# Expert weight loads in runs of 8 KB per partition instead of two runs of 4 KB

## What is computed

```python
def expert_block(args):
    xb, e = args                                    # up to 128 tokens of one expert, width 1024
    hb = jax.nn.silu(xb @ w_gate[e]) * (xb @ w_up[e])
    return hb @ w_down[e]
```

## Time and profile before

| | |
|---|---|
| median of three executions | 1955.79 us (1955.04 to 1960.65) |
| the profiled execution, its own time | 1958.94 us |
| its span, first to last instruction | 1957.3 us |
| mean granted TensorE clock | 0.979 of full speed |
| PE busy | 1833.4 us (94%) |
| DVE busy | 1338.2 us (68%) |
| ACT busy | 847.4 us (43%) |
| DMA moved in all | 610.26 MB, mean 312 GB/s |

### The profile page before, as it was taken

How to read it: one execution, slowest core, us unless ns; L and a number is a source line. 1 busy time by engine, 2 the same in 40 slices (tenths; PEclk the granted TensorE clock), 3 DMA queues, 4 the chain that set the end, 5 groups by cost and what they waited for, 6 DMA issues and landing times.

```text
span 1957.3 us, 22496 instructions
## 1 busy us (share of the span) xinstructions
PE 1833.4 (94%) x8664; PEld 1306.3 (67%) x8664; DVE 1338.2 (68%) x1527; ACT 847.4 (43%) x939; POOL 222.8 (11%) x260
## 2 busy tenths in 40 slices
PE   7999999999999998889889998999999898889896
PEld 3788657778888656545657677578776566556654
DVE  4776679998789646534657888777696456445656
ACT  2324623223357535433546454444465345434553
POOL 3000110102032010001010200100020110011001
PEclk9999999999999999999999999999999999999998
DMA  9776426667399999999999777186699999999995
GB/s 351 271 238 242 136 74 197 241 218 278 112 345 363 410 409 407 402 406 403 398 402 361 282 260 270 41 290 248 224 376 388 409 409 408 407 402 399 400 389 208
DMA packets 179902, 610.26 MB, mean 312 GB/s; under 512 B 17001, under 2 KB 19253, under 8 KB 172753
## 3 DMA queue, kind: packets, MB, share of 16 engines
q1 hardware_dynamic: 150648, 503.62, 67.3%
q0 software_dynamic: 26192, 100.40, 14.6%
q10 hardware_dynamic: 2952, 4.77, 0.7%
HBM read 593.78 MB, written 27.33 MB: 317 GB/s over the span
## 4 chain that ended last, share of the span: by engine, by line
PE 72%; DMA 13%; DVE 10%; ACT 3%; issue 1%; SPq 1%; POOL 0%; ACTq 0%; DVEq 0%; POOLq 0%
PE bank L2641 62%; DMA ring<-in_w_exp_down_dram 9%; PE bank L3124 5%; PE bank L2651 3%; DVE work L1773 3%; DVE w_lo L1773 2%; ACT w_hi L1628 1%; DMA ring<-in_w_mod_dram 1%; DMA work<-hp_dram 1%; DVE m_lo L1773 1%; PE bank L2914 1%; DVE ring L1773 1%; DMA work<-in_w_mod_dram 1%; DMA x<-in_ctx_dram 1%; DMA ring<-in_w_out_dram 1%
## 5 line engine op out<-in xcount | busy, mean ns | idle before, releaser
L1773 DVE TENSOR_TENSOR w_lo<-ring,w_hi 128x2048 fp32r<-128x2048 f32 x228 | 519.4, 2290 | 273.4 <-ACT w_hi L1628 272.8
L1628 ACT ACTIVATE w_hi<-ring 128x2048 fp32r<-128x2048 f32 x228 | 436.9, 1919 | 238.0 <-PE bank L2641 131.1
L1352 ACT ACTIVATE m_hi<-ring 128x1024 fp32r<-128x1024 f32 (+1 forms) x128 | 130.0, 1031 | 265.2 <-PE bank L2641 223.1
L2641 PE MATMUL bank<-w_hi,xsT_hi 128*128 128x512 f32 x608 | 238.0, 391 | 3.5 <-DVE w_lo L1773 1.7
L2641 PE MATMUL bank<-w_lo,xsT_hi 128*128 128x512 f32 x608 | 236.8, 389 | 0.0
L3124 PE MATMUL bank<-ring,mixed 128*64 128x512 f32 x832 | 185.4, 598 | 7.8 <-DMA ring<-in_w_exp_up_dram 7.8
L1773 DVE TENSOR_TENSOR m_lo<-ring,m_hi 128x1024 fp32r<-128x1024 f32 (+1 forms) x128 | 148.8, 1188 | 57.3 <-ACT m_hi L1352 55.7
L2641 PE MATMUL bank<-w_hi,xsT_lo 128*128 128x512 f32 x608 | 187.3, 389 | 0.0
L2641 PE MATMUL bank<-m_lo,hT_hi 128*128 128x512 f32 (+1 forms) x496 | 186.3, 376 | 0.0
L2641 PE MATMUL bank<-w_hi,hexpT_hi 128*128 128x512 f32 x304 | 131.4, 432 | 56.0 <-DVE w_lo L1773 56.0
L2641 PE MATMUL bank<-m_hi,hT_hi 128*128 128x512 f32 (+1 forms) x448 | 170.5, 380 | 6.3 <-DVE m_lo L1773 4.4
(11 more groups left out here) (322 smaller groups left out, 2810.1 us busy)
## 6 DMA issues: line engine op xcount, KB each, us to landing
ring<-in_w_exp_gate_dram SPq DMA_DIRECT2D x128, 1024.0 KB, 12.9
ring<-in_w_exp_up_dram SPq DMA_DIRECT2D x128, 1024.0 KB, 13.3
ring<-in_w_exp_down_dram SPq DMA_DIRECT2D x128, 1024.0 KB, 12.6
ring<-in_w_in_dram SPq DMA_DIRECT2D x44, 1024.0 KB, 6.8
work<-in_w_mod_dram POOLq DMA_DIRECT2D x40, 1024.0 KB, 5.5
work<-hp_dram SPq DMA_DIRECT2D x54, 256.0 KB, 4.5
work<-mod_dram POOLq DMA_DIRECT2D x8, 1024.0 KB, 9.8
ring<-in_w_out_dram SPq DMA_DIRECT2D x8, 1024.0 KB, 5.3
```

The lines of the kernel that those rows point to most:

```text
L1352: nc.scalar.activation(high_of(key, q)[:, 0:n], ring[:, cols], ACT.Copy).then_inc(split_hi, 1)
L1628: nc.scalar.activation(w_hi[:, n % N_HIGH, :], raw(slot_of(n)), ACT.Copy).then_inc(hi_done, 1)
L1773: return nc.vector.tensor_tensor(o, a, b, op)
L2641: return nc.tensor.matmul(o, a, b, start=first, stop=last)
```

## The change

The source of a quarter is read as 256 rows in neighbouring pairs: rows 2p and 2p + 1 go to partition p, as one run of 8 KB that is contiguous in HBM and in SBUF. A quarter is then contiguous over all partitions. The weight block k of a quarter in the slot now has the rows of parity k. The transposed tokens and hidden rows have to match this, so the transposes of `xs` and `hexp`, and the matmuls of `place_first`, take every second column of a stretch of 256 (`paired`). The number and order of instructions on every engine stay as they are: PE, ACT, DVE, POOL and SP run the same lists.

```diff
@@ quarter_w
             rows = slice(2 * P * q, 2 * P * (q + 1))
             if isinstance(e, int):
-                return A[name][l, e, rows, :].rearrange("(k p) n -> p k n", k=2)
-            return A[name][l, bass.ds(e, 1), rows, :].rearrange("o (k p) n -> p (o k) n", k=2)
+                return A[name][l, e, rows, :].rearrange("(p k) n -> p (k n)", k=2)
+            return A[name][l, bass.ds(e, 1), rows, :].rearrange("o (p k) n -> p (o k n)", k=2)
@@ load, on SP
-                    sp.dma_start(raw(i).rearrange("p (k n) -> p k n", k=2),
+                    sp.dma_start(raw(i),
                                  quarter_w(l, EXPERT_W[p // 4], expert_in(e if p < 8 else e - 1), p % 4))\
                         .then_inc(slot_loaded[i], 16)
@@ on PE
+            def paired(row, j):
+
+                return row[:, 2 * P * (j // 2) + j % 2:2 * P * (j // 2 + 1):2]
+
+            def turn_paired(dst, src):
+
+                for j in range(4):
+                    ins = nc.tensor.transpose(dst[:, j * P:(j + 1) * P], paired(src, j), ident)
+                return ins
@@ turn_xs
-                        turn(bank[at + half], xs[:, par, half * 512:(half + 1) * 512], 4).then_inc(xt_mm, 1)
+                        turn_paired(bank[at + half], xs[:, par, half * 512:(half + 1) * 512]).then_inc(xt_mm, 1)
@@ place_first
-                                ins = mm(bank[2 + half][:, j * P:(j + 1) * P], h2row[k][:, kk * P:(kk + 1) * P],
+                                ins = mm(bank[2 + half][:, j * P:(j + 1) * P], paired(h2row[k], kk),
                                          place[0][:, k, :], k == 0, k == nt - 1)
@@ turn_h
-                        turn(bank[6 + half], hexp[:, half, :], 4).then_inc(ht_mm, 1)
+                        turn_paired(bank[6 + half], hexp[:, half, :]).then_inc(ht_mm, 1)
```

## The result

The changed kernel takes 1938.08 us in the median of four runs (1934.74 to 1941.83), against 1955.49 us (1955.04 to 1960.65) for the kernel before on the same chip. The figures in brackets are the lowest and the highest run. The medians differ by 17.4 us. The ratio, which goes by all runs, is 0.9906 with a 95% interval of 0.988 to 0.9931, that is 18.4 us less (13.5 to 23.5): under 1%, but clear of the noise. The forecast was 1931 us, 24.7 us less.

A forecast was written before the change was run, and what follows sets the result against it. The prediction took the DMA rate in the two expert stages as the bound. Saving 24.7 us on loads, with transposes and gather at nothing, gave 1934.2 us from the profiled 1958.9, or 1931 us against the median; range 1923 to 1940.

The forecast's parts named there:

- The bound: Expert stages, 605 to 996 and 1485 to 1877 us: DMA rate sets the pace, PE waits 15 us per pair.
- The mechanism: Weight loads in the expert stretches: each packet saved by 8 KB runs takes off 10.6 ns, raising 409 GB/s to 423.
- Rival A: Expert-stage loads: rate hardly rises, 423 GB/s belonging to the kernel's start; gain 0 to 8 us, 1948 to 1956; chance 0.12.
- The size of that term: Loads in both expert stretches: 0.085 us less per quarter over 290.4 quarters, 24.7 us less.
- The dips stay: Expert stretches: short rate dips come with gathers, scatters and other traffic and remain, so 24.7 us is taken, not 37.
- rival C: Expert stretches: dips shrink too, with fewer packets in play; 37 us less, 1918 us; chance 0.06.
- The transposes at nothing: Transposes' weight loads reading every second float: priced at nothing; upper end 140 ns more each, 30 us in all.
- the prediction's own sign: Weight load of `bank<-const,mixed`: stays at 140 ns; at 200 or more rival B holds and stretches outside the stage lengthen.
- rival B: 212 exposed loads outside the stretches: strided loads eat the gain; at 0.14 us each 1961 us, half slower 1946; chance 0.08.
- The gather: POOL's token gathers beside longer packets: up to 1.2 us more on 7.6 us, 20 us free, priced at nothing.
- 3 cycles per packet: Skill page's fixed packet cost on the DMA engine's bus: 3.5 ns per packet, 8 us in all; forecast used measured rates.
- The sum: Whole kernel: 1958.9 less 24.7 is 1934.2 us; against the median of three, 1931 us.

The follow-up runs named there:

- e1: Changed kernel with the two rows of each pair swapped in the slot, so packets are 4 KB again, strided transposes kept; 1958.57 us, ratio 1.0012 to the kernel before.
- m1: Separate kernel without the computation, streaming weights on SP's queue with various run lengths and depths; 387, 410, 422, 429 GB/s for 2, 4, 8, 16 KB.
- a0: The changed kernel run once more, no edit; 1940.17 us against 1956.85 for the kernel before, ratio 0.991.
- e5: Changed kernel with eight raw slots for quarters instead of nine; 1948.24 us, ratio 0.9958 to the kernel before.
- m2: Separate kernel without the computation, making 64 transposes or plain float32 matmuls per column step; transposes 7.0 us at step 1, 7.8 at step 2.
- e7: Changed kernel with runs of 16 KB, 2 MB per transfer into two neighbouring slots, eight slots in four pairs; 2055.09 us, ratio 1.0512 to the kernel before.

## Why the prediction was right, point by point, and where its size was off

- **The bound.** Right. The chain still goes through a down quarter in every pair, PE still waits there, and e1 shows that time follows the rate of the loads. But the reading that PE "has some 50 us of its own work in a pair and waits 15" is wrong: it took the DMA piece of the chain, which starts with the issue, for PE's wait. PE is busy for 59.6 us of a pair and idle for 6.0. The forecast held all the same, since the 2.0 us to be saved in a pair are less than 6.0 too; after the change 4.6 are left.
- **The mechanism, a fixed cost for each packet.** Right: e1 takes back the length of the run alone and the gain is gone; m1 gives one rate for each length, wherever the rows lie. Rival A, that 423 GB/s belongs to the start of the kernel, fell with the 420 GB/s of the stage.
- **The size of that term**, 0.085 us for a quarter and 24.7 us in all, was too large; this is the main slip. The step "423 GB/s against 409" took its upper figure from 9 us. Over long windows the loads alone give 422 against 410, 0.073 us and 21.1 us in all; in the stretches themselves the pair of profiles gave 10.7 + 10.1 = 20.8 us, and a0's 19.3. So 4 to 5 of the 6 to 8 us by which the forecast was off are here. The windows were to show 421 to 424 GB/s and show 420. That pairs take just the forecast 63.5 us is partly luck: 24 quarters at 0.073 us are 1.8 us, and 2.1 were saved; in a0's profile a pair takes 63.8.
- **The dips stay** (rival C had them shrink). Right: the wide phases are 2.4% under the full rate of 410 before, and 2.2% under 422 after. e5 shows that part of them is a short queue, since with eight slots the wide phases are at 407 instead of 413. How much comes from single slow packets was not separated.
- **The transposes at nothing** was wrong, though small: the price is 2.3 us (0.6 to 4.1) by e1. By the prediction's own sign ("if it reads 200 or more, B holds") rival B would have won, as the load reads 209 ns; yet the kernel is faster, and the piece behind 996 us, which was to become longer, is 1.9 us shorter. The sign was badly chosen: the length of a load is not its price. Rival B's upper end, 140 ns for each exposed load, was far off, as loads overlap. It also counted two kinds of load as one: of the 212, 116 are transposes, at 12 ns each by m2, and 96 are plain loads of `place_first`, at (15.2 - 14.4) / 128 = 6 ns each. That is 1.4 + 0.6 = 2.0 us, in line with e1. The Trainium skill, page "SBUF — State Buffer", note on SBUF cachelines, says that two hits in a line of 16 bytes are enough for full speed. For the plain load m2 agrees, with 196 ns at step 2 against 192. For the load of a transpose it takes 209 ns instead of 140, so there the measurement decides against it.
- **The gather.** Right, in its mechanism too. It was to land 1.2 us later and stay covered; it lands 9.2 us after its issue instead of 7.6, 1.6 later, and no gather is on the chain of the stage before or after. The cover is not endless: with runs of 16 KB (e7) the median for wide experts is 13.1 us, and one gather is on the chain, with 15.66 us.
- **The Trainium skill's 3 cycles per packet**, page "DMA: Bandwidth & Descriptors", section "Why small descriptors are slow (HBM only)", are an estimate of 3.5 ns at the 850 MHz of that page's section "Where 436 GB/s comes from". The first section names a second fixed cost, 32 bytes of descriptor metadata for each operation, which the estimate leaves out; at the 423 / 16 = 26 GB/s of one engine that is an estimate of 1.2 ns more. m1 shows 9 to 10 ns for each packet; the trace does not agree with the page, and the gain of 8 us that follows from the 3 cycles alone fell.
- **The sum.** Not closed to the microsecond. The stretches gave 20.8 us in one pair of profiles and 19.3 in the other, and what of the stride's price lies inside them is already in that. Taking off all of e1's 2.3 us leaves 17 to 18.5 us, against 17.6 and 18.4 by the two ratios; the agreement is closer than the intervals (13.5 to 23.5 in the first) can support, and single profiles vary by some 5 us in the mixer of layer 0.

## What to carry to other kernels

Where a row of the profile shows DMA engines busy all the time and PE waiting for loads, the length of the contiguous run per partition is worth measuring: price it with long windows of a transfer of that length, if the kernel has one somewhere, as this one had in its `w_mod` loads. Lay the data out so that the other side pays in work that is hidden; here strided transposes cost 2 us and the runs gave 20. Don't buy longer runs with coarser or fewer slots: one slot less cost 9 to 13 us, half or more of what doubling the run gave, and 16 KB runs in four large slots made the kernel 5% slower. And don't read a DMA piece of the chain as the time for which PE waits: here it was 15 us, and the wait 6.

## What the runs showed of the hardware

- Rate of loads from HBM on one queue, with nothing else running on the core: 387, 410, 422 and 429 GB/s for runs of 2, 4, 8 and 16 KB, with no difference between one contiguous piece and rows that lie apart (halves 512 KB apart at 4 KB, pieces 192 KB apart at 8 KB).
- Three 1 MB transfers in flight hold the full rate when nothing else runs, two don't (387 GB/s with 4 KB, 369 with 8 KB); in the kernel, with some four queued, the rate is still 2% short during the wide phases.
- An indirect gather beside such loads takes longer to land the longer their packets are: for wide experts 7.6, 9.2 and 13.1 us beside runs of 4, 8 and 16 KB, for narrow ones 7.5, 9.1 and 9.5 (the last of each beside transfers of 2 MB).
- The weight load of a float32 transpose takes 140 ns with neighbouring columns, 209 at a step of 2 or 4, 198 at 3 and 187 at 8. The plain float32 load takes 192, 196 and 329 ns at steps 1, 2 and 4: a step of 2 is all but free for it, a step of 4 takes 71% more, and the stream of matmuls takes twice as long (29.9 instead of 14.4 us), where the transposes at step 4 lose a tenth.
